# A one-core transformer kernel: the per-layer embedding's projection, the expert ranks and the first expert selection change their place in block 1

## The reference, cut to what matters

```
mix = concat([y_mla, y_diff, y_sb]) @ w_o[i]
h   = layer_norm(ALPHA * h + mix, ln1_g[i], ln1_b[i])
ffn = grouped_moe(h, router_w, router_b, w_gate[i], w_up[i], w_down[i])
ple = sigmoid(h @ ple_gate[i]) * (p[i] @ ple_proj[i])
h   = layer_norm(ALPHA * h + ffn + ple, ln2_g[i], ln2_b[i])
```

## Time and profile before

| what | value |
|---|---|
| median of three runs | 1660.37 us (1655.16 to 1660.71) |
| profiled execution, span from first to last instruction | 1654.3 us, granted TensorE clock 0.989 of full |
| PE busy | 1560.4 us (94%), 9677 matmul rows |
| DVE busy | 801.9 us (48%) |
| ACT busy | 552.2 us (33%) |
| DMA | 346.65 MB, mean 210 GB/s |

### The profile page before, as it was taken

How to read it: one execution, slowest core, us unless ns; L and a number is a source line. 1 busy time by engine, 2 the same in 40 slices (tenths; PEclk the granted TensorE clock), 3 DMA queues, 4 the chain that set the end, 5 groups by cost and what they waited for, 6 DMA issues and landing times.

```text
span 1654.3 us, 23883 instructions
## 1 busy us (share of the span) xinstructions
PE 1560.4 (94%) x9677; PEld 1120.5 (68%) x9677; DVE 801.9 (48%) x1710; ACT 552.2 (33%) x1015; POOL 0.5 (0%) x7
## 2 busy tenths in 40 slices
PE   7998999999999999999989989899999989899999
PEld 5856655444486765544447667878999974598997
DVE  6897711111344671111126277684665636665444
ACT  3444211111224521111122355423443421644444
POOL 0000000000000000000000000000000000000000
PEclk9999999999999999999999999989999999999999
DMA  9532589999952458999991000308334534013552
GB/s 329 187 128 66 180 322 429 429 429 427 361 190 88 146 188 320 430 428 428 428 367 62 1 1 2 105 1 305 138 136 185 203 133 163 10 52 107 199 203 76
DMA packets 83728, 346.65 MB, mean 210 GB/s; under 512 B 8240, under 2 KB 15280, under 8 KB 71360
## 3 DMA queue, kind: packets, MB, share of 16 engines
q1 hardware_dynamic: 76272, 338.28, 52.2%
q10 hardware_dynamic: 7376, 7.26, 1.5%
HBM read 344.48 MB, written 1.05 MB: 209 GB/s over the span
## 4 chain that ended last, share of the span: by engine, by line
PE 42%; DVE 4%; ACT 2%; issue 1%; DMA 1%; DVEq 0%; ACTq 0%
PE ps L813 41%; DVE ring L2411 1%; DMA ring<-in_w_ff 1%; PE ps L1326 1%; DVE ring L2417 1%; DVE ring L2414 0%; ACT ring L2192 0%; DVE arena L2906 0%; DVE small L2908 0%; PE ps L1551 0%; DVE arena L2414 0%; DVE small L2902 0%; ACT ring L2194 0%; DVE ring_r L2411 0%; ACT arena L1794 0%
## 5 line engine op out<-in xcount | busy, mean ns | idle before, releaser
L813 PE MATMUL ps<-ring,arena 128*64 128x512 f32 (+6 forms) x1728 | 378.2, 574 | 20.3 <-DMA ring<-in_w_up 12.0
L813 PEld LDWEIGHTS ps<-ring,arena 128*64 128x64 f32 (+2 forms) x1728 | 136.6, 142 | 244.2 <-issue 239.2
L813 PE MATMUL ps<-arena_r,ring_r 128*128 128x272 f32 (+1 forms) x896 | 255.7, 285 | 0.0
L1794 ACT ACTIVATE arena<-ps 128x512 f32<-128x512 f32 (+7 forms) x161 | 73.3, 479 | 389.0 <-PE ps L813 194.1
L813 PEld LDWEIGHTS ps<-arena_r,ring_r 128*128 128x128 f32 x896 | 168.7, 188 | 0.0
L813 PE MATMUL ps<-arena_r,y_r 128*128 128x272 f32 (+1 forms) x560 | 157.5, 287 | 4.9 <-ACT arena L2332 2.4
L813 PE MATMUL ps<-h_r,y_r 128*128 128x272 f32 (+1 forms) x528 | 150.4, 285 | 0.0
L813 PE MATMUL ps<-arena_r,ff_hi_r 128*128 128x272 f32 (+1 forms) x576 | 119.7, 290 | 1.4 <-DVE hT L2411 1.4
L2417 DVE SCALAR_TENSOR_TENSOR arena<-arena,small,ps 128x512 f32<-128x512 f32 x16 | 12.0, 747 | 223.1 <-PE ps L813 223.1
L2411 DVE TENSOR_TENSOR ring_r<-ring,y_r 128x1024 fp32r<-128x1024 f32 x74 | 88.9, 1222 | 44.8 <-ACT y_r L1794 44.8
L813 PEld LDWEIGHTS ps<-arena_r,y_r 128*128 128x128 f32 x560 | 104.6, 189 | 7.1 <-ACT arena L2332 2.9
(11 more groups left out here) (329 smaller groups left out, 2258.3 us busy)
## 6 DMA issues: line engine op xcount, KB each, us to landing
ring<-in_w_down SPq DMA_DIRECT2D x32, 2048.0 KB, 13.3
ring<-in_w_gate SPq DMA_DIRECT2D x32, 2048.0 KB, 15.9
ring<-in_w_up SPq DMA_DIRECT2D x32, 2048.0 KB, 17.2
ring<-in_w_ff SPq DMA_DIRECT2D x32, 2048.0 KB, 9.0
ring<-in_w_in SPq DMA_DIRECT2D x8, 2048.0 KB, 19.3
ring<-in_w_in_ab SPq DMA_DIRECT2D x5, 2048.0 KB, 12.9
ring<-in_w_o SPq DMA_DIRECT2D x4, 2048.0 KB, 10.3
ring<-in_ple_gate SPq DMA_DIRECT2D x4, 2048.0 KB, 7.9
```

The costliest lines, as they stand in the source:

```text
L813: return pe.matmul(o, lhsT, rhs, start=a, stop=z)
L1794: return act.activation(o, i, ACT.Copy, scale=scale)
```

## The change

The arithmetic is the same. What moves, in each of the two layers of block 1:

- The transposes of `p` (`turn_embedding`) stand before tile 1 of `y @ w_o` and write bank 3; ACT copies them to `p_T` right after it has loaded the table of the square root, before the layer norm's first root.
- Of the four groups of `p @ ple_proj` (`embedding(half, t)`) two take the place of `stay_busy(2, 3)`, one that of `stay_busy(7, 2)`, and the fourth stands behind unit 1 of the product with `ple_gate`. They are counted by a semaphore of their own, `proj_mm`.
- The router's result goes to bank 7, the turned scores to bank 2, and `rank()` writes bank 0 and stands behind unit 5 of the product with `ple_gate`.
- `pick` gets its own place in memory (column 13568 of the arena), so that `select` can run inside the product.
- On DVE `embedded(g)` (product with the sigmoid) is apart from `residual(g)`: two before the ranks, two after `select`. The memsets of `got_lo` and `pickT` and all four residuals stand behind the copies of the first gather.
- The zeros for banks 0 to 3 stand behind `slot_gates` of the first round.
- `ple_gate`'s halves are in slots 2 and 5 (were 2 and 3). The first loads of the experts are issued in the order of slots 3, 0, 1, 4, 2, 5 (was 5, 0, 1, 2, 3, 4), with the second half of `ple_gate` behind slot 3.

```diff
-        pick = view(2048, NT * 2 * CAP, pat="p (t n) -> p t n", t=NT)
+        pick = view(13568, NT * 2 * CAP, pat="p (t n) -> p t n", t=NT)
+        PLE_SLOT = (2, 5)
@@ SP
-                first_free = [(mix_mm, 4 * l + 3), (mix_mm, 4 * l + 4), (ple_mm, 8 * l + 2), (ple_mm, 8 * l + 4),
-                              (ple_mm, 8 * l + 8), (u_mm, NU * l + U_LAST[5])]
-                for n in (5, 0, 1, 2, 3, 4):
+                first_free = [(mix_mm, 4 * l + 3), (mix_mm, 4 * l + 4), (ple_mm, 4 * l + 2), (u_mm, NU * l + U_LAST[3]),
+                              (proj_mm, 4 * (l + 1)), (ple_mm, 4 * l + 4)]
+                for n in (3, 0, 1, 4, 2, 5):
...
+                    if n == 3:
+                        gate_of_embedding(1)
@@ PE
+                def turn_embedding():
+                    pe.wait_ge(p_load, 16 * 3 * (l + 1))
+                    for c in range(2):
+                        for t in range(NT):
+                            ins = pe.transpose(ps[:, 3, c * S + t * P:c * S + (t + 1) * P], p_tok[:, t, c * P:(c + 1) * P], ident)
+                    ins.then_inc(ppT_mm, 1)
+                def embedding(half, t):
+                    wp = ring[:, 4 * SLOT_W:4 * SLOT_W + 2 * DM].rearrange("p (k n) -> p k n", n=DM)
+                    for k in range(2):
+                        ins = mm(ps[:, 4 + 2 * half + t, :], p_T[:, k, t * P:(t + 1) * P], wp[:, k, half * 512:half * 512 + 512], k == 0, k == 1)
+                    ins.then_inc(proj_mm, 1)
...
-                stay_busy(2, 3)
+                pe.wait_ge(ppT_ev, l + 1)
+                pe.wait_ge(slot_full[4], fullx(l, 4))
+                embedding(0, 0)
+                embedding(1, 0)
                 normed_tile(2 * l, 1)
-                stay_busy(7, 2)
+                embedding(0, 1)
...
                         if u == 1:
                             turn_scores()
+                            embedding(1, 1)
+                        if u == 5:
+                            rank()
@@ ACT
                 load_root_table(2 * l)
+                act.wait_ge(ppT_mm, l + 1)
+                copy(p_T.rearrange("p c s -> p (c s)"), ps[:, 3, :]).then_inc(ppT_ev, 1)
                 normed_feature_major(2 * l, 3 * l + 2)
@@ DVE
+                embedded(0)
+                embedded(1)
+                dve.memset(got_hi.bitcast(F32), 0.0)
                 dve.wait_ge(rank_mm, l + 1)
...
-                nothing_got()
                 select(0, 0)
+                embedded(2)
+                embedded(3)
...
                     gates_of_slots(R * (PAIRS + 1) + 1)
+                    if type(r) is int:
+                        nothing_got(True)
+                        for g in range(4):
+                            residual(g)
```

More of the change, by code:

```diff
@@ L305, in ple_unit @@
         def ple_unit(of, u):
[L306 to L307 removed]
+            n, q = PLE_SLOT[u // 4], u % 4
+            return of[:, n * SLOT_W:(n + 1) * SLOT_W].rearrange("p (k n) -> p k n", k=KC)[:, 2 * q:2 * q + 2, :]
         def wo_unit(of, u):
@@ L693, in _, with gate_of_embedding @@
                     sp.dma_start(slot(half, KC), A["w_o"][l].rearrange("(k p) n -> p k n", p=P)[:, :, half * 512:half * 512 + 512]).then_inc(slot_full[half], 16)
-                for half in range(2):
-                    sp.wait_ge(u_mm, NU * l + U_LAST[2 + half])
-                    sp.dma_start(slot(2 + half, KC), A["ple_gate"][l].rearrange("(k p) n -> p k n", p=P)[:, :, half * 512:half * 512 + 512]).then_inc(slot_full[2 + half], 16)
+                def gate_of_embedding(half):
+                    n = PLE_SLOT[half]
+                    sp.wait_ge(u_mm, NU * l + U_LAST[n])
+                    sp.dma_start(slot(n, KC), A["ple_gate"][l].rearrange("(k p) n -> p k n", p=P)[:, :, half * 512:half * 512 + 512]).then_inc(slot_full[n], 16)
+                gate_of_embedding(0)
                 sp.wait_ge(u_mm, NU * l + U_LAST[4])
@@ L1120, in _ @@
                         ins.then_inc(ple_mm, 1)
[L1121 to L1137, removed]
                 pe.wait_ge(h_final, NT * (2 * l + 1))
@@ L2060, in _ @@
                 act.wait_ge(rt_mm, 2 * l + 1)
-                act.activation(scores_T, ps[0:NE, 4, 0:S], ACT.Sigmoid).then_inc(rt_ev, 1)
+                act.activation(scores_T, ps[0:NE, 7, 0:S], ACT.Sigmoid).then_inc(rt_ev, 1)
                 ple_high(6)
                 ple_high(7)
-                act.wait_ge(ppT_mm, l + 1)
-                copy(p_T.rearrange("p c s -> p (c s)"), ps[:, 5, :]).then_inc(ppT_ev, 1)
                 act.wait_ge(ln_used, 2 * l + 1)
@@ L2769, in _, with embedded @@
                         gl.unsqueeze(2).to_broadcast([P, NT, NE]), ALU.mult))
+                def embedded(g):
+                    half, t = g // 2, g % 2
+                    dve.wait_ge(proj_mm, 4 * (l + 1))
+                    dve.wait_ge(ple_ev, 4 * l + g + 1)
+                    c = slice(half * 512, half * 512 + 512)
+                    tt(ple_sig[:, t, c], ple_sig[:, t, c], ps[:, 4 + g, :], ALU.mult).then_inc(acc_init, 1)
+                embedded(0)
+                embedded(1)
+                dve.memset(got_hi.bitcast(F32), 0.0)
                 dve.wait_ge(rank_mm, l + 1)
@@ L2788, in select, with nothing_got @@
                     ins.then_inc(sel_ready, 1)
-                def nothing_got():
+                def nothing_got(first):
                     dve.memset(pickT_r.bitcast(F32), 0.0)
-                    dve.memset(got_lo.bitcast(F32), 0.0)
-                    dve.memset(got_hi.bitcast(F32), 0.0).then_inc(got0_ev, 1)
+                    if not first:
+                        dve.memset(got_hi.bitcast(F32), 0.0)
+                    dve.memset(got_lo.bitcast(F32), 0.0).then_inc(got0_ev, 1)
                     dve.memset(rope_m[:, 0:1], 0.0).then_inc(got1_ev, 1)
-                nothing_got()
                 select(0, 0)
+                embedded(2)
+                embedded(3)
                 def residual(g):
@@ L2803, in residual @@
                     stt(acc[:, t, c], h[:, t, c], ALPHA, ple_sig[:, t, c], ALU.mult, ALU.add).then_inc(acc_full, 1)
-                for g in range(4):
-                    half, t = g // 2, g % 2
-                    dve.wait_ge(ple_mm, 8 * l + 4 + g + 1)
-                    dve.wait_ge(ple_ev, 4 * l + g + 1)
-                    c = slice(half * 512, half * 512 + 512)
-                    tt(ple_sig[:, t, c], ple_sig[:, t, c], ps[:, 4 + g, :], ALU.mult).then_inc(acc_init, 1)
-                    if g > 0:
-                        residual(g - 1)
-                residual(3)
                 def gathered(n):
```

39 lines of the change are left out of this document (21 added, 18 removed).

## The result

| | before | changed |
|---|---|---|
| runs of the first comparison, median | 1659.88 us (1655.16 to 1660.71, 4 runs) | 1646.45 us (1646.00 to 1648.79, 4 runs) |
| changed / before, 95% interval | | 0.992 (0.9908 to 0.9932) |
| first repeat, median | 1659.45 us (29 runs) | 1647.84 us (6 runs), 0.9926 (0.9913 to 0.9939) |
| second repeat, median | 1658.32 us (9 runs) | 1647.44 us (5 runs), 0.994 (0.9922 to 0.9957) |
| span of the profiled execution | 1654.3 us | 1644.2 us |

The change makes the kernel 11 to 13 us faster; the forecast was 11.3 us and 1649.1 us. The profiled execution of the changed kernel took 1646.0 us, 1.8 us more than its span.

What follows compares the result with a forecast made beforehand. PE, 94% busy, was taken as the bound, the expert weight stream hanging on the first expert's product. 8.65 less 3.0 gave 5.65 us a layer, 11.3 in two: 1660.4 to 1649.1 us, range 1643 to 1656.

Steps and rivals of the forecast that it cites:

- The tail: From the ranks to the first expert's product: ranks and projection leave, 13.89 to 5.24 us, 8.65 less a layer.
- The 0.74 us wait: Wait for DVE's copy of the second gather before the first expert's product; counted at nothing beside slot gates and zeros.
- The product with `ple_gate`: It takes in the fourth projection group and the ranks, 3.0 us more a layer, with no wait for the picks.
- Around the layer norm: Three projection groups replace idle time and constants around the second normed tile; 0.5 us to spare, router's start unmoved.
- The added waits: New waits on PE, ACT and DVE cost nothing; ACT's p_T copy has half a microsecond of cover, at most 0.6 us late.
- The sum: First expert's product 5.65 us earlier a layer, bounds 4.6 to 6.4; two layers 11.3 us, bounds 9.2 to 12.8.
- The moments: First expert's product at about 206.4 and, in layer 1, 614.5; second pair's gate loads at 213.7.
- A: Around the layer norm, the second normed tile is 0.6 to 2 us late a layer; gain 7.4 us, 1653 us; chance 0.12.
- B: In the expert stage, transfers swallow the gain because the stream could start no earlier; 1660 us; chance 0.07.
- C: PE stands before the projection's first group, the clock falls before the product with ple_gate; 1671 us; chance 0.05.
- The sign that the prediction named: In the changed trace, a granted clock below 1.00 after 165 would show the forecast wrong.
- The stretch of the earlier trace: Granted clock 0.83 of full in 140 to 150, after PE was busy 6.5 of 10 us; cost put at 1.7 us.

Runs made afterwards that it cites:

- the filler: Changed kernel with unused products in front of the output projection, where PE stood idle; median 1647.36 us, against 1647.44 us for the changed kernel beside it.
- new slots: Kernel before with only the exchange of ring roles (ple_gate in slots 2 and 5, first loads 3, 0, 1, 2, 5, 4); median 1660.30 us.
- no constants: Kernel before without both stay_busy calls around the layer norm's second normed tile; median 1659.91 us.
- the experiment that keeps the projection out of the gap: Changed kernel with all four projection groups inside the product with ple_gate and constants again around the layer norm; median 1658.14 us.
- the padded tail: Changed kernel with four unused f32 products between slot gates and zeros of the first round; median 1654.90 us.
- old slots: Changed kernel with ple_gate back in slots 2 and 3 and first loads in the order 5, 0, 1, 4, 2, 3; median 1659.14 us.
- ranks at the tail: Changed kernel with rank() again behind the product with ple_gate; median 1655.05 us.
- the early ranks with the new slots: Changed kernel with all four projection groups back behind the product with ple_gate, constants around the layer norm, ranks still inside; median 1660.79 us.

## Why the prediction was right, point by point

*The tail.* Forecast 13.89 to 5.24 us, measured 5.12. The 0.74 us wait is gone as argued: the copy ends at 205.64 + 0.69 = 206.33, before the last product with zeros ends.

*The product with `ple_gate`.* Forecast 3.0 us more, measured 2.96. The group inside it and the ranks wait for nothing: the ranks load at 193.12, forecast 192.7, and layer 0 as a whole is 0.5 us late. The selection is ready 5 us before the gather. Layer 0's timeline:

```profile
190.49 0.18 DVE L2776 COPY small<-small 128x32 f32<-128x32 f32 x1
...
193.12 0.42 PEld L820 LDWEIGHTS ps<-small,consts 128*128 128x128 f32 x2
...
195.46 0.73 DVE L2428 TENSOR_SCALAR arena<-consts,small 128x64 f32<-128x64 f32 x4
```

*Around the layer norm.* Forecast 0.5 us of idle time left, measured 0.47. From M of layer 1 to the first product with `ple_gate` it is 16.97 us before (572.79 to 589.76) and 16.56 after (569.04 to 585.60): 0.41 less, the transposes to the hundredth, so the projection cost nothing there.

*The added waits.* ACT's copy of `p_T` had its place, though the cover was as thin as said:

```profile
153.81 0.60 PE L1066 MATMUL ps<-consts,arena 128*128 128x128 f32 x4
154.44 0.60 ACT L1808 ACTIVATE arena<-ps 128x512 f32<-128x512 f32 x1 [0.79 <-PE ps L1066]
155.70 0.29 ACT L1832 ACTIVATE small<-small 128x1 f32<-128x1 f32 x1 [0.66 <-DVE small L2707]
```

It ends at 155.04, and the root that follows waits 0.66 us for DVE, not for it. I had the end at 154.7.

*The sum.* 5.65 us a layer was forecast and 5.8 measured, inside 4.6 to 6.4. That the first comparison's median (1646.45 us) lies 2.7 us below the forecast is chance of the runs more than mechanism: the repeats give 11.6 and 10.9 us, on either side of the forecast's 11.3. The moments were forecast less well than the differences: the first expert's product at 206.4 and 614.5, measured 206.76 and 615.84; the loads G at 213.7, measured 214.03. Layer 0 is late by 0.5 us from something ahead of M. Layer 1 loses another 1.1 us on the way from G of layer 0 to its M (355.01 us against 353.49, with the 0.41 us of the transposes in it). In these two profiles the loss is at the end of layer 0's expert stage. There PE stands 2.2 us for the address of a round in both kernels; before,

```profile
413.45 11.83 PE L813 MATMUL ps<-ring,arena 128*64 128x512 f32 x54 [2.21 <-SPq L734]
```

and in the changed kernel:

```profile
407.63 15.62 PE L820 MATMUL ps<-ring,arena 128*64 128x512 f32 x64 [2.22 <-SPq L741]
```

A row of the same product takes 11.83 / 54 = 0.219 us in the one and 15.62 / 64 = 0.244 in the other, and the windows over it, before and then after, have a granted clock of 1.00 and 0.94:

```profile
400.00:430.00 30.00, 27.79 (x148) 13.64 (x146) 3.13 (x6) 3.26 (x6) 0.00 (x0) 1.00 0.93 393
```

```profile
400.00:430.00 30.00, 26.82 (x120) 10.07 (x118) 2.13 (x3) 2.66 (x5) 0.00 (x0) 0.94 0.88 360
```

This is why the two spans differ by 10.1 us and not by 11.6; from G of layer 1 to the end both take the same, 1021.2 and 1021.1 us. The place of the loss belongs to these two executions: in both repeats the clock is 1.00 from 400 to 430, and G to M still takes 355.51 and 355.14 us, now with the low clock ahead of M that the filler showed. Kernels with the order of before took 353.86 (new slots) and 357.21 us (no constants). One profile of each can't tell whether a part of this 1 us belongs to the change. The medians differ by 13.4, 11.6 and 10.9 us, around 2 x 5.8 = 11.6, and show no such loss.

*The rivals.* A (the gap does not hold the projection) fell with the 0.47 us and with the experiment that keeps the projection out of the gap. B (the transfers swallow the gain) fell with the padded tail, where 3.53 us a layer came out as 7 us or a little more. C (the clock) did not occur in the changed kernel where it was priced: the window 165 to 216 has

```profile
165.00:216.00 51.00, 50.45 (x237) 32.79 (x238) 33.17 (x82) 14.01 (x20) 0.00 (x0) 1.00 0.58 205
```

The sign that the prediction named, a clock below 1.00 after 165, did occur to the letter, with the 0.94 of 400 to 430; that is in the expert stage, and it cost 1.6 us of that one execution. The stretch of the earlier trace rows, which I had put at 1.7 us, cost about half of that: from the first product of `y @ w_o` to M it is 18.33 us in layer 0 before (140.69 to 159.02), and 17.43 in layer 1 (555.36 to 572.79), where the clock was up. Of the 1.32 us of idle time in the layer norm the prediction said that the clock of the expert stage speaks for their being harmless; the window that bears on it is the one right behind, 176 to 184 of before, and its clock is 1.00 too.

But the mechanism of C is real, and was seen where the change is done by halves: with old slots and with the ranks at the tail. I had tied it to a missing filler in the layer norm, where it costs little, and had not looked for it at the tail, where nothing covers it. That the ranks and the first loads wait for nothing was right; the price if it had been wrong is 1.5 to 2.5 times the wait itself (3.47 and 3.71 us of waiting cost 5.2 and 6.7, 2.13 and 1.94 cost 3.8 and 4.8).

## What to carry to other kernels

Find the one moment that starts the transfer-bound stage, and count what PE does just ahead of it; work there that needs nothing of the chain (here a product of two inputs) goes where the engine already stands or runs fillers, and only there does it save its whole time. Several small edits can be worth nothing each and everything together, because each removes the wait that the others uncover: undo them one at a time from the finished version, not only add them one at a time to the old one. Here the new slots alone gave 1660.3 us, the early ranks with the new slots 1660.8, all without the new slots 1659.1, all without the early ranks 1655.1, and all together 1646.5 to 1647.8. Price a new wait of TensorE on a critical stretch at more than its own length.

## What the runs showed of the hardware that I had not expected

The clock fell to 1.2 GHz behind idle time of TensorE in several places: 1.94 us (gather with late ranks, layer 1, 0.50 of full behind it), 3.47 us (first experts with old slots, 0.66) and 3.90 us (layer norm without constants, 0.57). But it is not certain: the same 2.2 us in front of a round was followed by a granted clock of 1.00 before and 0.94 after, and the idle 2.02 and 2.16 us ahead of `y @ w_o` in layer 0 by 0.83 over 10 us before and by 1.00 in the changed kernel's first profile (below). In layer 1, with 0.47 and 2.16 us of idle time there, it was 1.00 over the first 10 us in that profile and 0.83 in both repeats.

```profile
140.00:150.00 10.00, 7.57 (x32) 5.93 (x33) 9.86 (x11) 10.00 (x12) 0.00 (x0) 1.00 0.31 71
```

The prediction drew on the Trainium skill's HAM oscillation (TensorE: Matmul & The Clock Gate), that PE idling in waits drops to the low clock and pays in the next burst; the rows of the two half-done versions agree with it. What a low stretch costs depends on who sets the pace behind it: 0.9 us of M at the start of `y @ w_o`, where DVE sets a part of it, and 2.9 us in the late gather, where PE sets all. Where the low stretches fall from run to run, and so part of the spread of 1653.6 to 1664.6 us among the runs of before, is left open: I have the profiled execution of each kernel only, not of each run.
